# Sparse attention walks its heads twice: tokens 0 to 383, then the last 128, whose keys VectorE selects beside the first walk

## What is computed

```
topk = min(TOPK_MAX, S // 4)                      # 512 // 4 = 128
score = einsum('bths,bth->bts', relu(s_idx), wi_b)
score = where(key_pos <= t_pos, score, -inf)
_, sel = lax.top_k(score, topk)
kv_sel = c_kv[sel]
logits = einsum('bthc,btkc->bhtk', q_abs, kv_sel) * qk_scale + bias[t5_bucket(dist)]
logits = where(dist >= 0, logits, -inf)
p = softmax(logits, axis=-1)
o_lat = einsum('bhtk,btkc->bthc', p, kv_sel)
o = einsum('bthc,hcv->bthv', o_lat, w_uv)
```

## Time and profile before

| | us |
|---|---|
| median of 3 runs (2181.28 to 2186.12) | 2182.88 |
| the profiled execution's own time | 2182.14 |
| its span in the trace | 2180.3 |
| TensorE busy (matmuls) | 2031.5 |
| VectorE busy | 1272.3 |
| ScalarE busy | 819.9 |
| GpSimd busy | 252.6 |

### The profile page before, as it was taken

One profiled execution on the slowest core, in us unless ns is written; L12 is line 12 of the kernel. 1 busy time (PEld: TensorE's weight loads), 2 busy tenths in 40 slices (PEclk: granted clock), 3 DMA queues, 4 the chain that ended last, 5 costly groups with the idle time before them and its releaser, 6 DMA issues. The chain is left out here.

```text
span 2180.3 us, 31787 instructions
## 1 busy us (share of the span) xinstructions
PE 2031.5 (93%) x13414; PEld 1559.8 (72%) x13414; DVE 1272.3 (58%) x1876; ACT 819.9 (38%) x1215; POOL 252.6 (12%) x175
## 2 busy tenths in 40 slices
PE   7999999999989997898899999999939899999998
PEld 3877767887767853787578888885516577888886
DVE  2335756665545477674577666434676367666535
ACT  3454654444333354323242222322426543222323
POOL 0000003324420003212400000000035100000000
PEclk9999999999999998999999999999969999999999
DMA  7323002211223310000212222223200022222221
GB/s 288 97 87 108 1 1 78 85 51 59 87 77 93 97 61 2 4 4 20 66 61 97 97 97 97 97 97 111 85 1 1 11 68 97 97 97 97 90 97 46
DMA packets 47023, 158.36 MB, mean 73 GB/s; under 512 B 5329, under 2 KB 7505, under 8 KB 46881
## 3 DMA queue, kind: packets, MB, share of 16 engines
q1 hardware_dynamic: 45296, 151.84, 21.3%
q10 hardware_dynamic: 1584, 4.49, 0.7%
HBM read 154.17 MB, written 2.14 MB: 72 GB/s over the span
## 5 line engine op out<-in xcount | busy, mean ns | idle before, releaser
L1043 PE MATMUL banks<-up_x_high,up_w_high 128*128 128x512 f32 x1056 | 411.7, 390 | 6.6 <-DVE up_w_low L1037 3.9
L1045 PE MATMUL banks<-up_x_high,up_w_low 128*128 128x512 f32 x1056 | 411.2, 389 | 0.0
L1044 PE MATMUL banks<-up_x_low,up_w_high 128*128 128x512 f32 x1056 | 411.2, 389 | 0.0
L1037 DVE TENSOR_TENSOR up_w_low<-weight_ring,up_w_high 128x1024 fp32r<-128x1024 f32 x132 | 161.6, 1225 | 268.7 <-ACT up_w_high L1032 268.7
L1032 ACT CAST up_w_high<-weight_ring 128x1024 fp32r<-128x1024 f32 x132 | 138.3, 1049 | 362.6 <-PE banks L1045 338.3
L1043 PEld LDWEIGHTS banks<-up_x_high,up_w_high 128*128 128x128 f32 x1056 | 198.2, 188 | 51.2 <-issue 9.5
L1045 PEld LDWEIGHTS banks<-up_x_high,up_w_low 128*128 128x128 f32 x1056 | 198.3, 188 | 41.3
L1044 PEld LDWEIGHTS banks<-up_x_low,up_w_high 128*128 128x128 f32 x1056 | 198.3, 188 | 40.8
L1579 POOL TENSOR_TENSOR hproj_w_low<-weight_ring,hproj_w_high 128x1024 fp32r<-128x1024 f32 x43 | 105.5, 2454 | 495.5 <-ACT hproj_w_high L1379 495.5
L1098 DVE SCALAR_TENSOR_TENSOR act<-banks,cols,act 128x511 f32<-128x511 f32 (+1 forms) x176 | 131.8, 749 | 6.2
L1254 PE MATMUL banks<-hproj_x_high,hproj_w_high 128*128 128x512 f32 x224 | 90.0, 402 | 5.2 <-DVE hproj_x_low L1530 3.4
(11 more groups left out here) (475 smaller groups left out, 3998.1 us busy)
## 6 DMA issues: line engine op xcount, KB each, us to landing
weight_ring<-in_up SPq DMA_DIRECT2D x88, 512.0 KB, 3.3
weight_ring<-in_down SPq DMA_DIRECT2D x44, 512.0 KB, 3.3
weight_ring<-in_w_ada SPq DMA_DIRECT2D x24, 512.0 KB, 5.7
weight_ring<-in_w_rkv SPq DMA_DIRECT2D x24, 512.0 KB, 3.6
weight_ring<-in_w_in SPq DMA_DIRECT2D x20, 512.0 KB, 3.7
weight_ring<-in_w_out SPq DMA_DIRECT2D x16, 512.0 KB, 3.5
weight_ring<-in_w_q SPq DMA_DIRECT2D x8, 512.0 KB, 4.6
weight_ring<-in_w_k SPq DMA_DIRECT2D x8, 512.0 KB, 3.6
```

Of the source, the lines that this page charges most:

```text
L1037: nc.vector.tensor_tensor(w_low[:, n % 2, :], ring[:, i % RING, :], w_high[:, n % 2, :].bitcast(f32), ALU.subtract).then_inc(wl_made, 1)
L1043: nc.tensor.matmul(PS[:, bank, :], high, x_high[:, k, :], start=start, stop=False)
L1044: nc.tensor.matmul(PS[:, bank, :], high, x_low[:, k, :], start=False, stop=False)
L1045: return nc.tensor.matmul(PS[:, bank, :], low, x_high[:, k, :], start=False, stop=stop)
```

## The change

The selection in the indexer block covers blocks 1 and 2 only, and only their masks are made there. The attention block then has 32 steps in place of 16 heads. Steps 0 to 15 are the 16 heads with query blocks 0, 2 and 1 (tokens 0 to 383, 768 columns); steps 16 to 31 are the 16 heads with block 3 alone (tokens 384 to 511, 512 columns). The 16 rounds of block 3's selection (`best_of_last`, `take_last`) stand in VectorE's program between the negation and the wait for the exponentials: one round in steps 0 to 4, 6, 8 and 10, two in steps 5, 7, 9 and 11. Block 3's mask is made in step 12, and GpSimd waits for it before step 16.

The logits get two sets of PSUM banks, (2, 3) and (4, 7) by turns, so that the logits of step s wait for the reads of step s - 2. The transposed probabilities take banks 5 and 6 (6 tiles) in the first walk, and bank 5 or 6 by turns (4 tiles) in the second. Copies and value products are cut to the walk's tokens. Arithmetic and results are the same; per head the matmuls' columns are the same in sum.

```
-        w_idx, best = small[:, 144:176], small[:, 176:208]
+        w_idx, best, best_last = small[:, 144:176], small[:, 176:208], small[:, 240:248]
+        LAST = NB - 1
...
-                    for b in range(1, NB):
+                    for b in range(1, LAST):
                         if k:
-                            dve.wait_ge(select, 6 * k - 3 + b)
+                            dve.wait_ge(select, 4 * k - 2 + b)
                         nc.vector.max(out=best[:, 8 * b:8 * b + 8], in_=left(b)[:, 0:(b + 1) * P]).then_inc(select, 1)
-                    for b in range(1, NB):
-                        dve.wait_ge(select, 6 * k + b)
+                    for b in range(1, LAST):
+                        dve.wait_ge(select, 4 * k + b)
                         nc.vector.match_replace(out=left(b)[:, 0:(b + 1) * P], in_to_replace=best[:, 8 * b:8 * b + 8],
                                                 in_values=left(b)[:, 0:(b + 1) * P], imm_value=TAKEN).then_inc(select, 1)
-                dve.wait_ge(select, 6 * (TOPK // 8))
-                for b in range(1, NB):
+                dve.wait_ge(select, 4 * (TOPK // 8))
+                for b in range(1, LAST):
...
-        TURN_OF = [0, 2, 1, 3]
+        BLOCKS = lambda s: (0, 2, 1) if s < H else (LAST,)
+        done = lambda s: LAST * min(s, H) + max(s - H, 0)
+        first_col = lambda s: 0 if s < H else LAST * P
+        tokens = lambda s: slice(0, LAST * P) if s < H else slice(LAST * P, T)
+        turned = lambda s, i, b: (0, T, LAST * P)[i] + (b - i) * P if s < H else i * P
+        n_turned = lambda s: 6 * P if s < H else T
+        ROUNDS = [1, 1, 1, 1] + [1, 2] * 4
+        assert sum(ROUNDS) == TOPK // 8
...
+                def logits(s):
+                    if s >= 2:
+                        pe.wait_ge(lg_masked, done(s - 1))
+                    for b in BLOCKS(s):
                         n = (b + 1) * P
-                        bank, at0 = LG_BANK[b]
-                        nc.tensor.matmul(PS[:, bank, at0:at0 + n], qabs[hh][:, b * P:(b + 1) * P], ckv_rev[:, T - n:T], start=True, stop=True).then_inc(lg_made, 1)
-
-                def turn(hh):
-                    pe.wait_ge(scaled, 4 * hh + 4)
-                    if hh:
-                        pe.wait_ge(pt_moved, hh)
-                    for i in range(NB):
-                        for b in range(i, NB):
-                            at0 = SB_AT[i] + (b - i) * P
-                            mm = nc.tensor.transpose(PS[:, 5 + at0 // T, at0 % T:at0 % T + P], lg[hh % 3][:, L_AT[b] + (b - i) * P:L_AT[b] + (b - i + 1) * P], mat("ident"))
+                        bank, at0 = logits_at(s, b)
+                        nc.tensor.matmul(PS[:, bank, at0:at0 + n], qabs[s % H][:, b * P:(b + 1) * P], ckv_rev[:, T - n:T], start=True, stop=True).then_inc(lg_made, 1)
...
+                def turn(s):
+                    pe.wait_ge(scaled, done(s + 1))
+                    if s:
+                        pe.wait_ge(pt_moved, s if s < H else max(H, s - 1))
+                    bank = 5 if s < H else 5 + s % 2
...
+                def best_of_last(r):
+                    if r:
+                        dve.wait_ge(last_selected, 2 * r)
+                    nc.vector.max(out=best_last, in_=left(LAST)).then_inc(last_selected, 1)
+
+                def take_last(r):
+                    dve.wait_ge(last_selected, 2 * r + 1)
+                    nc.vector.match_replace(out=left(LAST), in_to_replace=best_last, in_values=left(LAST), imm_value=TAKEN).then_inc(last_selected, 1)
...
+                    cols = slice(4 * p, 4 * p + LAST) if s < H else slice(4 * p + LAST, 4 * p + NB)
+                    dve.wait_ge(lg_masked, done(s + 1))
+                    nc.vector.tensor_scalar(nmx[:, cols], mx[:, cols], -1.0, None, ALU.mult).then_inc(negated, 1)
+                    if s < len(ROUNDS):
+                        for r in range(sum(ROUNDS[:s]), sum(ROUNDS[:s + 1])):
+                            best_of_last(r)
+                            take_last(r)
+                    if s == len(ROUNDS):
+                        dve.wait_ge(last_selected, 2 * sum(ROUNDS))
+                        nc.vector.tensor_scalar(mask[:, LAST, :][:, ::-1], left(LAST), TAKEN / 2, NEG, ALU.is_ge, ALU.mult).then_inc(last_mask, 1)
+                    dve.wait_ge(exped, done(s + 1))
+                    nc.vector.reciprocal(rs[:, cols], sm[:, cols]).then_inc(inverted, 1)
...
+                    if s == H:
+                        pool.wait_ge(last_mask, 1)
```

More of the change, by code:

```diff
@@ new lines, in turn @@
+                def turn(s):
[3 more added lines that the diff above has]
+                    bank = 5 if s < H else 5 + s % 2
+                    for i in range(LAST if s < H else NB):
+                        for b in sorted(BLOCKS(s)):
+                            if b >= i:
+                                at0 = turned(s, i, b)
+                                mm = nc.tensor.transpose(PS[:, bank + at0 // T, at0 % T:at0 % T + P], lg[s % 3][:, L_AT[b] + (b - i) * P:L_AT[b] + (b - i + 1) * P], mat("ident"))
+                    mm.then_inc(pt_made, 1)
@@ new lines, in latent @@
+                def latent(s):
+                    pe.wait_ge(pt_moved, s + 1)
+                    if s:
+                        pe.wait_ge(ol_moved, s)
+                    last_key = LAST - 1 if s < H else LAST
+                    for i in range(last_key + 1):
+                        first = max(i * P, first_col(s))
+                        at0 = turned(s, i, first // P)
+                        n = tokens(s).stop - first
+                        mm = nc.tensor.matmul(PS[:, 1, first:first + n], ckv_tok[:, i * P:(i + 1) * P], pt_[s % 2][:, at0:at0 + n],
+                                              start=i == 0, stop=i == last_key)
@@ L2792, in _ @@
                 logits(0)
                 logits(1)
[L2794 to L2803, removed]
+                for s in range(STEPS + 1):
+                    if s + 2 < STEPS:
+                        logits(s + 2)
+                    if s < STEPS:
+                        turn(s)
+                    if s >= 3 and s % 2:
+                        values((s - 3) // 2)
+                    if s:
+                        latent(s - 1)
@@ L2805, in _ @@
+                values(STEPS // 2 - 1)
             @block.vector
             def _(dve):
[L2807 to L2811, removed]
+                def best_of_last(r):
+                    if r:
+                        dve.wait_ge(last_selected, 2 * r)
+                    nc.vector.max(out=best_last, in_=left(LAST)).then_inc(last_selected, 1)
@@ L2812, in _ @@
+                def take_last(r):
+                    dve.wait_ge(last_selected, 2 * r + 1)
+                    nc.vector.match_replace(out=left(LAST), in_to_replace=best_last, in_values=left(LAST), imm_value=TAKEN).then_inc(last_selected, 1)
+                for s in range(STEPS):
+                    p = s % 3
+                    if s >= 3:
+                        dve.wait_ge(pt_made, s - 2)
+                    for i, b in enumerate(BLOCKS(s)):
                         n = (b + 1) * P
-                        bank, at0 = LG_BANK[b]
```

95 lines of the change are left out of this document (44 added, 51 removed).

## The result

The changed kernel's median is 2167.27 us of 5 runs (2157.11 to 2170.42), against 2182.88 us (2174.30 to 2186.12): ratio 0.9918 with a 95% interval of 0.9895 to 0.9940, so it is faster, by 0.8%. The forecast was 2167.0. I therefore read the stretches that it does touch.

The account below looks back on a forecast made before the run. Selection alone was the path before the barrier; then VectorE's ring and TensorE both bound the walk. Selection minus 20.5 us and walk 118.8 against 114.0 give back 15.7: 2182.1 becomes 2166.4, forecast 2167, range 2161 to 2177.

Parts of the forecast that it names:

- Selection: Indexer block before the barrier: 16 rounds lose their 512-key instructions and the widest mask goes, minus 20.5 us.
- First walk: Steps of 768 columns: masking, hand-over and exponentials, reciprocal and scaling on VectorE sum to 3.96 us a step.
- One round free: First walk: one moved round of 1.5 us fits the 1.82 us for which VectorE idles, so costs nothing.
- A second round: First walk, four steps with two rounds: 1.3 us more on VectorE's ring each, 5.2 us in all.
- Step 0: Start of the first walk: first mask 2.0 us after the barrier, then the step lasts 4.9 us.
- Second walk: Block 3 alone: TensorE becomes the bound by little, between 2.37 and 2.65 us a step, taken as 2.6.
- The ring: Second walk: VectorE's cycle through masking, negation, ScalarE's exponential, reciprocal and scaling, 2.37 us a step.
- Passage and end: Between the walks a wide latent product left, 1.0 us; chain after the last masking starts, 7.3 us.
- 4.8 us as the cost of cutting it in two: Attention walk: 118.8 us against 114.0, put down to 32 rings paying the fixed hand-overs that 16 paid.
- The half clock in the second walk: Rival: TensorE falls to 1.2 GHz there, steps take 5.2 us, 42 us more, 2209; 5 in 100.
- the weight loads: Rival: narrow matmuls bound by weight loads, second-walk step 3.5 us, 14 us more, 2181; 7 in 100.
- the rounds out of ScalarE's shadow: Rival: moved rounds come out at full price, 12 further ones add 18 us, 2185; 5 in 100.

Follow-up runs that it names:

- e1: Changed kernel with the walk cut in two but all three blocks still selected in the indexer block, no moved rounds: 2178.87 us, walk 113.41.
- e2: Changed kernel with the 16 moved rounds placed two to a step in steps 0 to 7: 2173.12 us, walk 122.26.
- e3: Changed kernel with only the first of four key blocks in the second walk's latent product: 2167.27 us, walk 114.51.
- e4: Changed kernel with VectorE scaling only the first 128 of 512 columns in the second walk: 2171.18 us, walk 117.58.
- e7: Changed kernel with ScalarE's latent copy placed ahead of the exponentials: 2165.32 us, walk 116.50.
- e10: The changed kernel itself, unedited, timed again beside e9: 2167.2 us, ratio 0.9918.
- e6: Changed kernel with one moved round ahead of step 0, one in each of steps 0 to 14, mask in step 15: 2166.92 us, walk 113.87.
- e8: Changed kernel with the edits of e6 and e7 together: 2164.09 us, ratio 0.9916, walk 112.70.
- e9: e8 with GpSimd's addition for step 17 waiting for the scaling of step 15: 2164.4 us, ratio 0.9911, walk 111.82.

## Why the prediction was right, step by step

**Selection, minus 20.5 us.** Measured 20.40 (48.84 less 28.44). Rounds of two blocks are 1.71 us apart, 1.70 expected.

**First walk.** A step of 3.96 us, measured 3.97, from the sum of masking, hand-over, exponentials and scaling. A moved round of 1.5 us, measured 1.51. One round free: e1 and the changed kernel have the same 3.97. A second round 1.3 us, measured 1.16: the first MAX8 starts 0.08 us after the negation and not 0.14, and the reciprocal starts at 1609.15 while the last replacement (1608.56, 0.68) still runs. e2 tells this from a price by number.

**Step 0.** Expected 2.0 and 4.9, measured 2.22 and 4.60 (first maskings at 1584.52 and 1589.12). The addition of GpSimd met the negation and not the scalings.

**Second walk.** TensorE as the bound at 2.6 us a step, by little; measured 2.47, shown by e3 and e4. The ring was put at 2.37 and e3 has it at 2.36. The price of the latent product in narrow matmuls, the open point, came out at 0.89 to 0.99 us, and the logits took 0.87 where 0.90 to 1.01 was the range. The prediction's terms for two steps gave 4.87 to 5.31; 4.94 lies near the lower end, and the 2.6 was taken too near the upper. The rule of the Trainium skill that transposes don't count for the clock (TensorE: Matmul & The Clock Gate, Part 4: PE-mode transpose) could have let the clock fall; the granted clock was 1.00 in every window of 4 us of the second walk. Whether they count no run here tells, since matmuls stand between them.

**Passage and end.** The passage was put at 1.0 us and took 1.8; the end was put at 7.3 and took 7.76 (from the last masking's start at 1692.17). The cause that I had left out is ScalarE's order: its copy of the latent product waits behind exponentials that wait for VectorE, so TensorE leaves the first walk behind schedule. e7 shows half of the passage's 1.8 us to be that (11.6 to 10.7, against 9.9).

**The walk as a whole.** 118.8 expected, 117.63 measured. My sum named 4.8 us as the cost of cutting it in two. That attribution failed. The sum itself held 5.2 us for doubled rounds, so by its own terms nothing was left for the cut, and e1 shows the cut walk without rounds 0.6 us shorter than the whole one. The reason given, fixed hand-overs paid 32 times and not 16, does show in the steps (6.44 us a head and not 6.11), but the shorter ends give it back.

**The sum.** Minus 15.7 us expected, minus 16.75 measured in the touched stretches, and minus 15.6 in the medians. That the medians agree within 0.1 us is partly luck, since executions of one kernel differ by 10 us and more; the stretches carry the proof. The profiled execution adds 11.1 us gained ahead of the selection and 2.8 lost behind the walk; the second trace of the same kernel (e10) has neither.

**The rivals.** The half clock in the second walk, the weight loads and the rounds out of ScalarE's shadow are all out. One statement was wrong: I expected a clock of 1.00 from the fourth step on. The argument was that both walks keep TensorE busier than a stretch that ran at 1.00. It fell to 0.57 between 1600 and 1604 in the changed kernel, where TensorE had waited 0.50 us and then stood in a wait of 2.42 us for ScalarE's copy. It cost nothing there, while e1 and e6 paid 0.4 to 0.5.

## What to carry to other kernels

Look for the idle time inside a ring of engines and put serial work of another stage there, in pieces no longer than the gap. A piece that fits is free, and one that doesn't costs what sticks out (here 1.16 of 1.51 us), so spread pieces one to a gap before doubling up. When work moves beside a pipeline, look also at what it releases late: a mask that came too late pushed one addition into another engine's scaling and cost 0.9 us. And judge a change of 1% by the stretches that it touches, with the medians as a check, when unchanged stages vary as much between executions.

## What the runs showed of the hardware

**VectorE's scaling stands still while GpSimd adds, and the selection does not.** The scaling took 1.78 us in e8 beside an addition and 0.88 in e9 without one. The first of its three instructions shows where the time goes, in e8 and then in e9:

```profile
1660.63 1.19 DVE L2867 TENSOR_SCALAR act<-act,small 128x128 f32<-128x128 f32 x1
...
1660.19 0.29 DVE L2867 TENSOR_SCALAR act<-act,small 128x128 f32<-128x128 f32 x1
```

It ends at 1661.82, just behind the addition (1660.46 + 1.27 = 1661.73). MAX8 and the replacement over 512 keys took 0.69 and 0.68 us in the changed kernel right beside an addition, and the addition took 2.09, as the walk's first one did with VectorE idle (1582.30):

```profile
1598.26 2.09 POOL L2876 TENSOR_TENSOR aux<-ffn_act,act 128x128 f32<-128x128 f32 x3 [1.88 <-DVE small L2847]
...
1598.29 0.69 DVE L2832 MAX8 small<-act 128x8 f32<-128x512 f32 x1
1599.01 0.09 DVE L2836 MATCH_VALUE_LOAD act<-small,act 128x8 f32 x1
1599.09 0.68 DVE L2836 MATCH_REPLACE8 act<-small,act 128x512 f32<-128x512 f32 x1
```

By the Trainium skill (SBUF — State Buffer, SBUF: two separate sides) VectorE and GpSimd share one pair of ports, taken for a whole instruction by whoever comes first, and on VectorE only certain operations need it. The traces agree: the scaling that came second took 1.19 in place of 0.29 us, and MAX8 and the replacement kept theirs.

**Unchanged stages vary by some 16 us between executions.** The first MAX8 came at 1553.86 to 1570.43 us in twelve traces that share all code ahead of it. In eleven of them it lies between 1562.26 and 1570.43; the earliest is the changed kernel's profiled execution. Much of its lead arises in the projection behind the recurrent stage. In the trace of before TensorE waited there and its clock fell (windows, columns as above):

```profile
1052.00:1056.00 4.00, 1.06 (x3) 0.19 (x1) 4.00 (x2) 1.10 (x2) 4.00 (x5) 0.89 0.00 0
1056.00:1060.00 4.00, 1.06 (x3) 0.90 (x4) 4.00 (x4) 0.00 (x0) 2.62 (x3) 0.50 0.00 0
```

and in the trace of the changed kernel it did not, in the same stage:

```profile
1044.00:1048.00 4.00, 3.96 (x13) 1.71 (x10) 4.00 (x7) 0.99 (x3) 4.00 (x4) 1.00 0.00 0
1048.00:1052.00 4.00, 4.00 (x19) 3.27 (x18) 2.19 (x3) 0.82 (x2) 4.00 (x4) 1.00 0.01 4
```

The wait in front of the projection's first matmul was 5.87 us before, none in the changed kernel's first trace and 7.36 in its second. What decides it stays open. In the same way the time behind the walk was 452.4 to 452.9 us in six traces and 454.8 to 455.4 in six, both values for the changed kernel itself. In its first trace the projection behind the walk ran at half clock for longer (windows, columns as above):

```profile
1704.00:1708.00 4.00, 4.00 (x11) 3.13 (x10) 0.85 (x2) 0.00 (x0) 0.00 (x0) 0.50 0.00 0
1708.00:1712.00 4.00, 4.00 (x16) 3.23 (x15) 0.00 (x0) 0.15 (x1) 0.00 (x0) 0.84 0.00 0
```

than in its second:

```profile
1720.00:1724.00 4.00, 4.00 (x15) 3.15 (x14) 0.68 (x2) 0.00 (x0) 0.00 (x0) 0.76 0.00 0
```

That accounts for 1.4 us of the 3.0 between these two traces, and it doesn't tell the two groups apart: e7 and e8 ran there at half clock for 6.8 us, as the changed kernel did in its first trace, and stayed at 452.8 and 452.9. What all six longer traces have and none of the shorter is a second fall of the clock, some 80 us behind the walk in the feed-forward stage, where TensorE had waited 1.93 us for VectorE's part of the weights (L1037). Here it is in the changed kernel's first trace (windows, columns as above); in its second the same stretch ran at 1.00:

```profile
1778.00:1782.00 4.00, 2.07 (x8) 1.54 (x7) 3.13 (x4) 1.97 (x2) 0.00 (x0) 0.87 0.69 260
1782.00:1786.00 4.00, 4.00 (x14) 3.13 (x14) 2.26 (x4) 1.56 (x2) 0.00 (x0) 0.70 0.01 2
```

What decides whether it comes stays open.
